# Experts ranked by token count: five passes of 96 slots and three of 64, written in line, rows returned once per round

## The chip, the cores and the metric

The kernel runs on one core of a Trainium2 chip. The metric is the device time of one execution in microseconds, median of several. The engines are TensorE (PE; its weight loads stand apart as PEld), VectorE (DVE), ScalarE (ACT), GpSimd (POOL) and SyncE (SP, which only issues DMAs). Each runs its own instruction stream, and they meet in semaphores.

## The reference

A trunk of two layers for 256 tokens of width 1024, all in float32. Layer 0 is windowed attention and a dense SwiGLU. Layer 1 is a Mamba-2 mixer and a mixture of experts, followed by a last norm. The change touches the mixture of experts alone:

```python
D_FF = 3584
N_EXPERTS = 8
TOP_K = 2
...
def moe_swiglu(h, w_router, w_gu, w_down):
    logits = (h @ w_router).astype(jnp.float32)
    top_v, top_i = lax.top_k(logits, TOP_K)
    gates = jax.nn.softmax(top_v, axis=-1)
    combine = jnp.sum(jax.nn.one_hot(top_i, N_EXPERTS, dtype=jnp.float32) * gates[..., None], axis=-2)
    ...
    for e in range(N_EXPERTS):
        out = out + combine[..., e:e + 1] * swiglu(h, w_gu[e], w_down[e])
    return out
```

The 512 choices (256 tokens, two each) are spread over eight experts. One expert's weights are 1024 x 7168 and 3584 x 1024 floats, 44 MB, and 352 MB for all eight.

## The kernel before

Up to about 562 us it runs layer 0 and the mixer of layer 1, with weights through a ring of six slots. Early in the dense SwiGLU, POOL clears two arrays in DRAM: `xg_rows`, the rows sent to the experts (L406), and `y_rows`, the rows that come back (L411). DVE waits for the clearing in front of L1731. Then comes the expert stage.

**The router** (DVE, L1817 to L1868) ranks the logits of each token and takes two. PE counts the tokens of each expert (L1233 to L1237). Each expert has 96 slots (`CAP`) in a round. Where one has more tokens, a second or third round of all eight experts follows; `last_i` says how many passes there are, less one. Every engine reads it into a register (L1249 on PE) and loops over the passes. The rows of expert 0 are picked by a matmul with a selection matrix (L1244), since nothing may wait for DRAM there; the others are scattered by POOL (L426) into `xg_rows`, and ACT loads those of the next expert in each pass (L741).

**A pass** (`expert`) handles one expert's 96 rows. The weights come as 48 chunks through `e_ring`, which has twelve slots of 128 x 2048 floats: 16 gate and up chunks of 1024 KB (set 0: 4 blocks of 512 columns), 16 of 768 KB (set 1: 4 blocks of 384), 12 down chunks of 1024 KB and 4 of 512 KB. SP issues the load of a chunk (L337) as soon as PE has used the one twelve before it (`chunk_used`). PE waits for a chunk on `e_loaded` (`have_e`).

The 96 rows are three groups of 32 (`QUAD`), and each matmul has 32 rows as its stationary side, at one of four positions of the array, so that four matmuls run beside one another. A gate or up chunk takes 12 matmuls (3 row groups x 4 blocks of columns), spread over three PSUM banks (L1283). A down k-tile takes 12 as well (L1301). The trace records each float32 matmul twice, so a pass has 768 records of L1283 and 672 of L1301. Between them PE transposes the hidden rows (L1274) and the next expert's rows (L1259); ACT does the Silu and moves the transposes, DVE multiplies gate by up (L1916), and both copy the down results to `yg`, which ACT stores to `y_rows` (L770).

**The loop.** All passes but the last are one loop body per engine (`Fori`; on PE L1341), and the last is written behind it. In the last pass POOL gathers the returned rows (L432 on) and DVE adds them with their gates (`rows_added`); the last expert's own rows stay in SBUF and come back by a matmul with `sel_last_T` (L1350). Then DVE adds that (L1947), ACT squares (L780), and the last norm follows. The vector of its gains, `gain_row`, is loaded in front of the last pass (L775).

Of the kernel before, what the change touches and what calls it, by code (L numbers as in the profile page):

```python
# [34 lines left out]
P = 128  # L35
T = 256
# [26 lines left out]
SLOT = 2048  # L63
CAP = 96
ROUNDS = -(-T // CAP)
QUAD = 32
# [4 lines left out]
CLEARED = ROUNDS * E * CAP // P + (ROUNDS - 1) * E + 1  # L71


def build(nc, x, positions, ln_mix, ln_ffn, ln_final, swa_w_qkv, swa_b_qkv, swa_sinks, swa_w_o,
# [11 lines left out]
    with ctx:  # L86
# [70 lines left out]
        first_slot = sb("first_slot", [P, TT, E])  # L157
# [26 lines left out]
        last_i = sb("last_i", [P, 1], I32)  # L184
        xg_rows = nc.dram_tensor("xg_rows", (ROUNDS * E, CAP, D), F32).ap()
        y_rows = nc.dram_tensor("y_rows", (ROUNDS * E, CAP, D), F32).ap()

# [47 lines left out]
        sel_last = cmp8[:].rearrange("p a t j -> p (a t j)").rearrange("p (t s) -> p t s", t=TT)[:, :, 0:CAP]  # L235
        sel_last_T = zeros[0:CAP, 0:T].rearrange("p (t s) -> p t s", t=TT)
# [10 lines left out]
        def at_quad(i):  # L247

            return slice(i % 4 * QUAD, (i % 4 + 1) * QUAD), i // 4, i // 3, slice(i % 3 * QUAD, (i % 3 + 1) * QUAD)
# [9 lines left out]
        def place_of(head):  # L259
# [31 lines left out]
        r_logit, r_max, r_exp, r_sel, r_cnt, r_passes, r_slots = map(  # L291
            sem, ("r_logit", "r_max", "r_exp", "r_sel", "r_cnt", "r_passes", "r_slots"))
# [9 lines left out]
        y_free, zeros_ready, rows_cleared = map(sem, ("y_free", "zeros_ready", "rows_cleared"))  # L302
# [9 lines left out]
        def _(sp):  # L312
# [53 lines left out]
        def _(pool_e):  # L366
# [11 lines left out]
            for i in range(NF):  # L378
                pool_e.memset(invf[:, i:i + 1], float(np.float32(THETA ** (-2.0 * i / ROT))))
            pool_e.iota(first_slot[:], [[0, TT], [CAP, E]], base=0, channel_multiplier=0,  # L380
                        allow_small_or_imprecise_dtypes=True)
# [18 lines left out]
            pool_e.wait_ge(f_gate, 1)  # L400
            pool_e.iota(column, [[1, P]], base=-int(FAR), channel_multiplier=0,
# [11 lines left out]
            pool_e.wait_ge(rows_cleared, 2 * CLEARED * 16)  # L413
# [15 lines left out]
            pool_e.wait_ge(r_passes, 1)  # L429
            last = pool_e.value_load(last_i[0:1, 0:1], min_val=E - 1, max_val=ROUNDS * E - 1)  # L430
            pool_e.sem_inc(y_free, 1)
            with pool_e.Fori(0, last) as it:  # L432
                pool_e.wait_ge(y_stored, it * 16 + 16)
                pool_e.sem_inc(y_free, 1)

            for i in range(2):
                if i == 1:
                    pool_e.wait_ge(y_added, TT)
                for t in range(TT):
                    pool_e.indirect_dma_start(xs[:, t], None, y_rows.rearrange("i p d -> (i p) d"),  # L440
                                              bass.IndirectOffsetOnAxis(slots_i[:, i, t:t + 1], 0)
                                              ).then_inc(y_got_in, 16)
# [3 lines left out]
        def _(act):  # L446
# [268 lines left out]
            act.wait_ge(r_passes, 1)  # L715
            last = act.value_load(last_i[0:1, 0:1], min_val=E - 1, max_val=ROUNDS * E - 1)
            act.sem_inc(y_act, 6)
            act.activation(root_table[:, 6:7], ones[:, 6:7], ACT.Silu)

            def expert(it, is_last):  # L720

                def gate(s, w):
                    act.wait_ge(chunk_used, it * LAYER_CHUNKS + (MOE0 + 16 * s + 8))
                    if s == 1:
                        act.wait_ge(m_h, 2 * it + 1)
                    for b in range(3):
                        ins = act.activation(m_sg[:, b, 0:w], bank[GATE[b]][:, 0:w], ACT.Silu)  # L727
                    ins.then_inc(m_silu, 1)

                def hidden_T(s, banks):  # L730
                    act.wait_ge(m_T, 2 * it + s + 1)
                    n = SETS[s][1] // P
                    for b in range(3):
                        ins = act.activation(m_hTs[s][:, :, b], bank[banks[b]][:, 0:n * P].rearrange("p (a n) -> p a n", a=n),  # L734
                                             ACT.Copy)
                    ins.then_inc(m_Tsb, 1)

                gate(0, 512)
                if not is_last:
                    act.wait_ge(rows_sent, 16 * 2 * TT)  # L740
                    act.dma_start(xg[0:CAP], xg_rows[it + 1]).then_inc(xg_loaded, 16)  # L741
# [3 lines left out]
                if is_last:  # L745
                    act.wait_ge(last_T, 1)
                    act.activation(sel_last_T, bank[UP[0]][0:CAP, 0:T].rearrange("p (t s) -> p t s", t=TT), ACT.Copy
                                   ).then_inc(last_sb, 1)
                    load_roots(4)
                else:  # L750
                    for i in range(2):
                        act.wait_ge(xg_T, it * 2 + (i + 1))
                        act.activation(xgT[:, 4 * i:4 * i + 4],
                                       bank[UP[i]][:].rearrange("p (a n) -> p a n", a=4)[:, :, 0:CAP],
                                       ACT.Copy).then_inc(xg_sb, 1)
                for b in range(3):
                    if b < 2:
                        act.wait_ge(m_y, it * 2 + (b + 1))
                    else:
                        act.wait_ge(chunk_used, it * LAYER_CHUNKS + (MOE0 + LAYER_CHUNKS))  # L760
                    if b == 0:
                        act.wait_ge(y_free, it + 1)
                    for q in (2, 3):
                        quad, _, d, rows = at_quad(4 * b + q)
                        act.activation(yg[rows, d * 256:(d + 1) * 256], bank[DOWN[b]][quad, 0:256], ACT.Copy  # L765
                                       ).then_inc(y_act, 1)
                if not is_last:
                    act.wait_ge(y_act, it * 6 + 12)
                    act.wait_ge(y_dve, it * 6 + 12)
                    act.dma_start(y_rows[it], yg[0:CAP]).then_inc(y_stored, 16)  # L770

            with act.Fori(0, last) as it:
                expert(it, False)
            act.wait_ge(rows_ready, TT)
            act.dma_start(gain_row, ln_final.partition_broadcast(P)).then_inc(gain_loaded, 16)  # L775
            expert(last, True)
            for n in range(2):
                for t in range(TT):
                    act.wait_ge(h_final, 2 * n + t + 1)
# [7 lines left out]
        def _(pe):  # L787
# [460 lines left out]
            pe.wait_ge(r_passes, 1)  # L1248
            last = pe.value_load(last_i[0:1, 0:1], min_val=E - 1, max_val=ROUNDS * E - 1)  # L1249

            def expert(it, is_last):
# [725 lines left out]
```

## Time and profile before

| | us |
|---|---|
| median of 3 runs | 1504.18 |
| lowest, highest | 1499.16, 1506.42 |
| the profiled execution | 1505.61 |
| its span, first to last instruction | 1503.8 |
| first matmul of an expert pass | 562.43 |
| first of the last products (L1350) | 1491.22 |

The profile is of one execution. Busy shares are of the span. "Issue" in the chain is time in which the engine waited for nothing that the profile shows. The granted clock is TensorE's, as a share of 2.4 GHz; the DMA share is the mean busy share of 16 DMA engines. The last column of a stretch is GB/s.

### The profile page before, as it was taken

Reading aid. Unit: us, or ns where it says so; the run is one execution under the profiler, and the core shown is the slowest. Engines: PE = TensorE matmul, PEld = TensorE weight load, DVE = VectorE, ACT = ScalarE, POOL = GpSimd, SP = SyncE. Lnnn points to the kernel's source line nnn. Section 1 sums busy time; section 2 is a strip of 40 time slices with the busy share of each in tenths; the row PEclk is TensorE's granted clock in tenths of the full one; section 3 lists DMA queues with packets and bytes.
Section 4 is the critical chain, followed back from the end, with each engine's and each line's share of the span. In section 5 each row is a group of like instructions: output and inputs, shape, how many; then the busy total and the mean of one; then the engine's idle time right before and its main releaser. Section 6 shows DMA issues by size and latency. Waiting matters only on the chain.

```text
span 1503.8 us, 33750 instructions
## 1 busy us (share of the span) xinstructions
PE 1461.4 (97%) x14996; PEld 863.8 (57%) x14996; DVE 427.8 (28%) x635; ACT 389.5 (26%) x590; POOL 81.8 (5%) x131
## 2 busy tenths in 40 slices
PE   8999999999999999999998999998999999999997
PEld 7688888888999873453462353353354344345344
DVE  6675554466899740000000000000000000001112
ACT  5654444346788530010000001000000000001011
POOL 2053000000012200000000000000000000000000
PEclk9999999999999999999999999999999999999999
DMA  9379855545544479999999999999999999999992
GB/s 336 120 271 409 314 182 185 190 157 169 160 121 141 141 266 378 371 397 397 359 405 375 345 414 399 343 410 383 337 405 396 362 407 391 371 400 387 423 419 109
DMA packets 132974, 471.55 MB, mean 314 GB/s; under 512 B 10080, under 2 KB 35952, under 8 KB 116448
## 3 DMA queue, kind: packets, MB, share of 16 engines
q1 hardware_dynamic: 123808, 440.44, 77.9%
q0 software_dynamic: 6624, 21.20, 3.6%
q10 hardware_dynamic: 2400, 7.70, 1.4%
q8 instruction: 127, 2.08, 0.5%
q14 instruction: 15, 0.12, 0.0%
HBM read 447.28 MB, written 22.02 MB: 312 GB/s over the span
## 4 chain that ended last, share of the span: by engine, by line
PE 82%; issue 12%; DVE 2%; POOLq 1%; DMA 1%; ACT 1%; DVEq 1%; SPq 0%; POOL 0%; ACTq 0%
PE bank L1283 39%; PE bank L1301 19%; PE bank L790 6%; PE bank L792 6%; PE bank L791 6%; PE bank L1274 1%; POOLq L421 1%; DMA ring<-swa_w_qkv_in 1%; DVE w_lo L1412 1%; POOLq L419 0%; PE bank L1012 0%; ACT w_hi L478 0%; PE bank L1259 0%; PE bank L815 0%; PE bank L1350 0%
## 5 line engine op out<-in xcount | busy, mean ns | idle before, releaser
L1283 PE MATMUL bank<-e_ring,xgT 128*32 128x512 f32 (+1 forms) x6144 | 591.9, 547 | 20.8 <-issue 20.8
L1283 PEld LDWEIGHTS bank<-e_ring,xgT 128*32 128x32 f32 x6144 | 198.4, 111 | 407.9 <-issue 407.6
L1412 DVE TENSOR_TENSOR w_lo<-ring,w_hi 128x2048 fp32r<-128x2048 f32 (+1 forms) x84 | 191.9, 2288 | 110.1 <-ACT w_hi L478 109.8
L478 ACT ACTIVATE w_hi<-ring 128x2048 fp32r<-128x2048 f32 (+1 forms) x84 | 158.8, 1895 | 127.4 <-PE bank L792 118.7
L1916 DVE TENSOR_TENSOR m_hh<-m_sg,bank 128x512 f32<-128x512 f32 (+1 forms) x48 | 26.9, 616 | 577.5 <-PE bank L1283 577.5
L1301 PE MATMUL bank<-e_ring,m_hT_a 128*32 128x256 f32 x3072 | 168.9, 379 | 0.0
L1301 PEld LDWEIGHTS bank<-e_ring,m_hT_a 128*32 128x32 f32 x3072 | 99.0, 110 | 67.2 <-issue 3.3
L790 PE MATMUL bank<-w_hi,hT_hi 128*128 128x512 f32 (+1 forms) x336 | 131.1, 390 | 2.1 <-DVE w_lo L1412 1.7
L792 PE MATMUL bank<-w_hi,hT_lo 128*128 128x512 f32 (+1 forms) x336 | 129.2, 384 | 0.0
L791 PE MATMUL bank<-w_lo,hT_hi 128*128 128x512 f32 (+1 forms) x336 | 129.1, 384 | 0.0
L1301 PE MATMUL bank<-e_ring,m_hT_b 128*32 128x256 f32 x2304 | 125.8, 379 | 0.0
L1301 PEld LDWEIGHTS bank<-e_ring,m_hT_b 128*32 128x32 f32 x2304 | 74.9, 110 | 49.4
L1938 DVE COPY yg<-bank 32x256 f32<-32x256 f32 x48 | 19.9, 415 | 276.5 <-PE bank L1301 275.8
L727 ACT ACTIVATE m_sg<-bank 128x512 f32<-128x512 f32 (+1 forms) x48 | 22.7, 545 | 241.3 <-PE bank L1283 241.3
L790 PE MATMUL bank<-hT_hi,w_hi 128*128 128x256 f32 x256 | 73.1, 286 | 0.9 <-DVE w_lo L1412 0.9
L790 PEld LDWEIGHTS bank<-w_hi,hT_hi 128*128 128x128 f32 x336 | 63.1, 188 | 16.2 <-DVE w_lo L1412 2.4
L792 PE MATMUL bank<-hT_hi,w_lo 128*128 128x256 f32 x256 | 72.4, 283 | 0.0
L791 PE MATMUL bank<-hT_lo,w_hi 128*128 128x256 f32 x256 | 72.4, 283 | 0.0
L734 ACT ACTIVATE m_hT_a<-bank 128x512 f32<-128x512 f32 x24 | 12.6, 599 | 225.5 <-PE bank L1274 225.5
L792 PEld LDWEIGHTS bank<-w_hi,hT_lo 128*128 128x128 f32 x336 | 63.1, 188 | 12.8
L791 PEld LDWEIGHTS bank<-w_lo,hT_hi 128*128 128x128 f32 x336 | 63.2, 188 | 11.9
L765 ACT ACTIVATE yg<-bank 32x256 f32<-32x256 f32 x48 | 18.1, 376 | 184.3 <-PE bank L1301 183.8
(330 smaller groups left out, 1232.8 us busy)
## 6 DMA issues: line engine op xcount, KB each, us to landing
e_ring<-moe_w_gu_in SPq DMA_DIRECT2D x128, 1024.0 KB, 7.4
e_ring<-moe_w_gu_in SPq DMA_DIRECT2D x128, 768.0 KB, 6.5
e_ring<-moe_w_down_in SPq DMA_DIRECT2D x96, 1024.0 KB, 10.8
ring<-ffn_w_gu_in SPq DMA_DIRECT2D x28, 1024.0 KB, 8.9
e_ring<-moe_w_down_in SPq DMA_DIRECT2D x32, 512.0 KB, 10.1
ring<-ffn_w_down_in SPq DMA_DIRECT2D x14, 1024.0 KB, 4.9
xg_rows<-zeros POOLq DMA_DIRECT2D x36, 256.0 KB, 12.3
ring<-ssm_w_in_in SPq DMA_DIRECT2D x8, 1024.0 KB, 5.0
```

The costliest lines, as they stand in the source:

```text
L421: pool_e.drain()
L478: act.activation(w_hi[:, m % SPLIT, 0:w], ring[:, m % RING, 0:w], ACT.Copy).then_inc(hi_ready, 1)
L727: ins = act.activation(m_sg[:, b, 0:w], bank[GATE[b]][:, 0:w], ACT.Silu)
L765: act.activation(yg[rows, d * 256:(d + 1) * 256], bank[DOWN[b]][quad, 0:256], ACT.Copy).then_inc(y_act, 1)
L790: pe.matmul(o, stat[0], mov[0], start=start, stop=False)
L791: pe.matmul(o, stat[0], mov[1], start=False, stop=False)
L792: return pe.matmul(o, stat[1], mov[0], start=False, stop=stop)
L1283: ins = pe.matmul(bank[banks[b]][quad, 0:w], xgT[:, k, rows], e_ring[:, c % ERING, block_n * w:(block_n + 1) * w], start=(k == 0), stop=(k ...
L1301: ins = pe.matmul(bank[DOWN[b]][quad, 0:256], hT_at[:, a, i // P, i % P:i % P + QUAD], e_ring[:, (32 + c) % ERING, (k - k0) * D + d * 256: ...
L1412: dve.tensor_tensor(w_lo[:, m % SPLIT, 0:w], ring[:, m % RING, 0:w], w_hi[:, m % SPLIT, 0:w].bitcast(F32), ALU.subtract).then_inc(lo_ready, 1)
L1916: ins = dve.tensor_tensor(m_hh[:, b, 0:w], m_sg[:, b, 0:w], bank[UP[b]][:, 0:w], ALU.mult)
L1938: dve.tensor_copy(yg[rows, d * 256:(d + 1) * 256], bank[DOWN[b]][quad, 0:256]).then_inc(y_dve, 1)
```

## The change

Experts are ranked on the chip by their token counts. Expert 0 always ranks first (its first chunks are loaded before the counts are known). The five that rank highest take passes of 96 slots, the other three passes of 64, which have two row groups in place of three. The passes stand in the set order of ranks 0, 5, 1, 2, 6, 3, 4, 7, so sizes are 96, 64, 96, 96, 64, 96, 96, 64. `order_i` tells SP which expert's weights each pass needs, `rounds_i` tells all engines how many rounds there are. The loop goes over rounds, and its body holds the eight passes in line. The returned rows are gathered and added once per round, in its last pass, so `y_rows` needs room for one round and less of it is cleared. `gain_row` is loaded before the loop. The last product sits in the loop, and ACT waits for all of `back_mm` before it leaves.

```diff
+SMALL = 64
+RANK_AT = (0, 5, 1, 2, 6, 3, 4, 7)
+LARGE = 5
+GROUPS = tuple(CAP // QUAD if r < LARGE else SMALL // QUAD for r in RANK_AT)
...
         @block.sync
...
-            sp.wait_ge(r_passes, 1)
-            last = sp.value_load(last_i[0:1, 0:1], min_val=E - 1, max_val=ROUNDS * E - 1)
+            sp.wait_ge(r_order, 1)
+            rounds = sp.value_load(rounds_i[0:1, 0:1], min_val=1, max_val=ROUNDS)
+            last = sp.snap(rounds * E - 1, min_val=E - 1, max_val=ROUNDS * E - 1)
             with sp.Fori(0, last) as it:
-                expert_loads(it, it % E, ERING, LAYER_CHUNKS)
-                expert_loads(it + 1, (it + 1) % E, 0, ERING)
-            expert_loads(last, E - 1, ERING, LAYER_CHUNKS)
+                here = sp.value_load(order_i[0:1, bass.ds(it % E, 1)], min_val=0, max_val=E - 1)
+                expert_loads(it, here, ERING, LAYER_CHUNKS)
+                following = sp.value_load(order_i[0:1, bass.ds(it % E + 1, 1)], min_val=0, max_val=E - 1)
+                expert_loads(it + 1, following, 0, ERING)
...
         @block.gpsimd
...
-            for i in range(E - 1, ROUNDS * E):
-                for a in range(2):
-                    pool_e.dma_start(y_rows[i][:, 512 * a:512 * (a + 1)], zeros[0:CAP, :]
-                                     ).then_inc(rows_cleared, 16)
...
+            for p in range(E):
+                filled = rows_of(p) if p < E - 1 else 0
+                if filled < CAP:
...
+            with pool_e.Fori(0, rounds) as it:
+                pool_e.wait_ge(r_back, it + 1)
+                pool_e.wait_ge(y_stored, it * (16 * (E - 1)) + 16 * (E - 1))
...
         @block.scalar
...
+            act.wait_ge(rows_ready, TT)
+            act.dma_start(gain_row, ln_final.partition_broadcast(P)).then_inc(gain_loaded, 16)
+            act.wait_ge(r_rounds, 1)
...
+            with act.Fori(0, rounds) as it:
+                for p in range(E):
+                    expert(it, p)
+                act.wait_ge(back_mm, it * (2 * TT) + 2 * TT)
...
         @block.tensor
...
                 def up_or_gate(c, s, banks):
                     w, k = SETS[s][1], c % 8
                     have_e(c)
-                    for b in range(3):
+                    for b in range(groups):
                         for q in range(4):
...
+                pe.wait_ge(xg_loaded, it * (16 * E) + 16 * (p + 1))
+                if p == E - 1:
+                    pe.wait_ge(last_ready, it + 1)
                 hidden_T(1, GATE)
-                if is_last:
+                if p == E - 1:
                     shares_T()
-                else:
-                    rows_T()
+                rows_T()
...
-            with pe.Fori(0, last) as it:
-                expert(it, False)
-            expert(last, True)
...
+            with pe.Fori(0, rounds) as it:
+                for p in range(E):
+                    expert(it, p)
+                pe.wait_ge(last_sb, it + 1)
+                pe.wait_ge(xg_sb, it * (2 * E) + (2 * E + 2))
...
+                pe.wait_ge(h_final, it * (2 * TT) + 4 * TT)
...
         @block.vector
...
+            dve.scalar_tensor_tensor(key, counts, float(E), key_bias[:], ALU.mult, ALU.add)
...
+            dve.tensor_reduce(rank, rank_is, AXX, ALU.add)
...
+            dve.tensor_scalar(small, rank, LARGE - 0.5, float(CAP - SMALL), ALU.is_gt, ALU.mult)
...
+            dve.tensor_scalar(rounds_i[:], rk[:, 8, 0:1], 1.0, None, ALU.add).then_inc(r_rounds, 1)
```

On PE, at the end of the first pass. Before, where L1301 are the last down matmuls and L1283 the next pass's first gate matmuls:

```order
L1301 MATMUL bank7<-e_ring,m_hT_b 32x256 x16
L1301 MATMUL bank5<-e_ring,m_hT_b 32x256 x16
L1341 REGISTER_ALU
L1341 COMPARE_AND_BRANCH
L1312 ISA
L1254 ISA
L1283 MATMUL bank0<-e_ring,xgT 32x512 x4
L1283 MATMUL bank1<-e_ring,xgT 32x512 x4
L1283 MATMUL bank2<-e_ring,xgT 32x512 x4
```

And now, with a pass of two row groups behind it:

```order
L1351 MATMUL bank7<-e_ring,m_hT_b 32x256 x16
L1351 MATMUL bank5<-e_ring,m_hT_b 32x256 x16
L1362 REGISTER_ALU
L1305 REGISTER_ALU
L1333 MATMUL bank0<-e_ring,xgT 32x512 x4
L1333 MATMUL bank1<-e_ring,xgT 32x512 x4
```

The branch is gone from between the passes, and a chunk has eight matmuls in two banks in place of twelve in three.

On DVE, between the selection of the first rows and the number that the loops wait for. Before:

```order
L1848 TENSOR_TENSOR rt<-rt 128x16
L1850 TENSOR_REDUCE rt<-bank0 128x1
L1852 TENSOR_SCALAR rt<-bank7 128x16 x2
L1854 TENSOR_TENSOR rt<-rt,st 128x16
L1856 TENSOR_SCALAR rt<-rt 128x1 x2
L1857 TENSOR_TENSOR rt<-rt,first_slot 128x16
L1858 TENSOR_TENSOR rt<-rt,bank7 128x16
L1860 TENSOR_TENSOR rt<-rt 128x1
L1861 TENSOR_TENSOR rt<-rt 128x16
L1863 TENSOR_SCALAR last_i<-rt 128x1
```

Now, from the ranks on (`rk` holds ranks, sizes and reaches):

```order
L1908 TENSOR_REDUCE rk<-cmp8 128x8
L1909 TENSOR_TENSOR rt<-rt,st 128x16
L1911 TENSOR_SCALAR rk<-rk 128x8
L1913 TENSOR_SCALAR choice<-rt 128x16 x2
L1915 TENSOR_TENSOR rk<-bank0,rk 128x8
L1916 TENSOR_TENSOR rt<-bank7,rk 128x16
L1918 TENSOR_TENSOR rk<-rk 128x8
L1919 TENSOR_SCALAR rk<-rk 128x8
L1921 SCALAR_TENSOR_TENSOR rk<-rk 128x8
L1923 TENSOR_REDUCE rk<-rk 128x1
L1925 TENSOR_SCALAR rounds_i<-rk 128x1
```

The ranking stands ahead of the number of rounds, and the order of the experts and the slots follow behind it.

On ACT, at the end of the program. Before, the squares stand right behind the last copies to `yg`:

```order
L765 ACTIVATE yg<-bank5 32x256 x2
L780 ACTIVATE xs,rt<-h 128x512 x4
```

Now the wait for the last products and the loop's branch stand between:

```order
L814 ACTIVATE yg<-bank7 32x256 x2
L824 ISA
L821 REGISTER_ALU
L821 COMPARE_AND_BRANCH
L827 ISA
L828 ACTIVATE xs,rt<-h 128x512
```

## Rows read from the trace of the kernel before

**Rows 1.** The page: busy shares; moved bytes in 40 equal slices

```profile
PE 1461.4 (97%) x14996; PEld 863.8 (57%) x14996; DVE 427.8 (28%) x635; ACT 389.5 (26%) x590; POOL 81.8 (5%) x131
...
GB/s 336 120 271 409 314 182 185 190 157 169 160 121 141 141 266 378 371 397 397 359 405 375 345 414 399 343 410 383 337 405 396 362 407 391 371 400 387 423 419 109
```

**Rows 2.** Busy time by stretch: passes 1, 2, 3, 8; passes 2 to 8

```profile
core 0: us, PE busy (x) PEld busy (x) DVE busy (x) ACT busy (x) POOL busy (x), PEclk, DMA share, GB/s
562.50:674.60 112.10, 112.09 (x1469) 49.39 (x1469) 5.48 (x11) 10.00 (x22) 3.97 (x4) 1.00 0.98 379
674.60:791.15 116.55, 113.85 (x1469) 50.42 (x1469) 5.86 (x12) 8.70 (x20) 0.00 (x0) 0.99 0.99 385
791.15:910.88 119.73, 114.80 (x1470) 49.09 (x1469) 5.86 (x12) 8.69 (x20) 0.00 (x0) 0.97 0.99 378
...
1379.71:1491.22 111.51, 111.51 (x1465) 48.87 (x1456) 12.43 (x27) 9.67 (x21) 3.83 (x4) 1.00 0.85 349
...
674.60:1491.22 816.62, 795.81 (x10278) 346.14 (x10278) 47.58 (x99) 61.81 (x141) 3.83 (x4) 0.98 0.98 379
```

**Rows 3.** Chain that ended last: start us, length us, what

```profile
674.59 2.71 issue
677.30 50.84 PE bank L1283 x480
729.60 23.36 PE bank L1283 x288
752.96 10.36 PE bank L1301 x192
765.12 26.04 PE bank L1301 x480
...
1379.71 48.94 PE bank L1283 x480
```

**Rows 4.** PE loop's branch by line; stretch behind the first jump back

```profile
L1341 PEldq COMPARE_BRANCH  x7: 83/3802/5972, 673.2 to 1378.4; - x7
...
678.60:682.00 3.40, 3.40 (x20) 0.90 (x16) 0.00 (x0) 0.00 (x0) 0.00 (x0) 0.50 0.96 360
```

**Rows 5.** Waits of SP in the expert stage: us in total, times, longest

```profile
SPq L337 <- PE bank L1283: 465.0, 256, 8.7
```

**Rows 6.** DMA from 1390 to 1470 us: 40 slices, packets, one group of issues

```profile
GB/s 436 414 434 418 422 422 434 412 429 425 421 423 421 421 433 421 424 429 415 417 422 421 426 417 418 419 422 422 416 410 426 422 420 420 412 418 422 414 420 422
DMA packets 7164, 33.71 MB, mean 421 GB/s; under 512 B 637, under 2 KB 637, under 8 KB 6499
...
e_ring<-moe_w_down_in SPq DMA_DIRECT2D x12, 1024.0 KB, 14.1
```

**Rows 7.** Busy time by stretch: two stretches of lower rate

```profile
674.60:690.00 15.40, 12.70 (x104) 3.90 (x108) 0.83 (x2) 0.75 (x2) 0.00 (x0) 0.89 0.98 386
...
1050.00:1100.00 50.00, 50.00 (x536) 17.54 (x532) 1.88 (x3) 4.41 (x9) 0.00 (x0) 1.00 0.97 347
```

**Rows 8.** DVE and PE by time at the router; PE's register load by line

```profile
558.07 0.16 DVE L1844 TENSOR_REDUCE rt<-rt 128x2 f32<-128x16 f32 x1
...
559.81 0.15 DVE L1863 TENSOR_SCALAR last_i<-rt 128x1 int32<-128x1 f32 x1
...
L1249 PEldq TENSOR_LOAD <-last_i x1: 485/485/485, 560.3 to 560.3; - x1
...
562.43 1.07 PE L1283 MATMUL bank<-e_ring,xgT 128*32 128x512 f32 x8
```

**Rows 9.** ACT's last squares by line: min/median/max ns, first and last start

```profile
L780 ACT ACTIVATE xs<-h x4: 629/630/630, 1493.0 to 1495.6; 128x512 f32<-128x512 f32 x4
```

**Rows 10.** Clearing of y_rows, and VectorE behind its wait, by line

```profile
L411 POOL DMA_DIRECT2D y_rows<-zeros x34: 512/512/555, 110.6 to 127.3; - x34
...
L1731 DVE TENSOR_SCALAR zeros<-arg,sm x1: 474/474/474, 383.8 to 383.8; 128x384 f32<-128x384 f32 x1
```

More of the change, by code:

```diff
@@ L763, in expert @@
+                for b in range(GROUPS[p]):
+                    if b < GROUPS[p] - 1:
+                        act.wait_ge(m_y, it * m_y_before(E) + (m_y_before(p) + b + 1))
+                    else:
+                        act.wait_ge(chunk_used, it * (E * LAYER_CHUNKS) + (MOE0 + (p + 1) * LAYER_CHUNKS))
+                    if b == 0 and p > 0:
+                        act.wait_ge(y_stored, it * (16 * (E - 1)) + 16 * p)
                     for q in (2, 3):
-                        quad, _, d, rows = at_quad(4 * b + q)
@@ L1279, in up_or_gate @@
                     have_e(c)
-                    for b in range(3):
+                    for b in range(groups):
                         for q in range(4):
-                            quad, _, block_n, rows = at_quad(4 * b + q)
+                            quad, _, block_n, rows = at_quad(p, 4 * b + q)
                             ins = pe.matmul(bank[banks[b]][quad, 0:w], xgT[:, k, rows],
@@ L1290, in down @@
                         have_e(32 + c)
[L1291 removed]
+                    for b in range(groups):
                         if chunks[0] == 0 and b == 2:
[L1293 removed]
+                            pe.wait_ge(m_h, it * (2 * E) + (2 * p + 2))
                         for c in chunks:
@@ new lines, in _ @@
+            dve.tensor_tensor(based, rank_is, base_at[:].unsqueeze(1).to_broadcast([P, E, E]), ALU.mult)
+            dve.drain()
+            dve.tensor_reduce(rk[:, 9], taken, AXX, ALU.add)
+            dve.tensor_reduce(base, based, AXX, ALU.add)
+            dve.tensor_scalar(r2[6], r2[6], CAP - 0.5, None, ALU.is_gt)
+            dve.tensor_scalar(step, small, float(ROUND_ROWS - CAP), None, ALU.add)
+            dve.drain()
+            dve.tensor_copy(order_i[:, 0:E], rk[:, 9])
+            dve.tensor_copy(order_i[:, E:E + 1], rk[:, 9, 0:1]).then_inc(r_order, 1)
@@ L1938, in expert @@
                         dve.tensor_copy(yg[rows, d * 256:(d + 1) * 256], bank[DOWN[b]][quad, 0:256]).then_inc(y_dve, 1)
-            with dve.Fori(0, last) as it:
-                expert(it, False)
-            expert(last, True)
-            for n in range(2):
-                for t in range(TT):
-                    dve.wait_ge(back_mm, 2 * n + t + 1)
-                    hh = h[:, t, 512 * n:512 * (n + 1)]
-                    dve.tensor_tensor(hh, hh, bank[2 * n + t][:], ALU.add).then_inc(h_final, 1)
+            with dve.Fori(0, rounds) as it:
+                for p in range(E):
+                    expert(it, p)
+                for n in range(2):
+                    for t in range(TT):
+                        dve.wait_ge(back_mm, it * (2 * TT) + (2 * n + t + 1))
+                        hh = h[:, t, 512 * n:512 * (n + 1)]
+                        dve.tensor_tensor(hh, hh, bank[2 * n + t][:], ALU.add).then_inc(h_final, 1)
```

359 lines of the change are left out of this document (208 added, 151 removed).

## The prediction

> **What bounds the kernel now.** I read the shares first. TensorE (PE) is busy for 97% of the span, and the moved bytes rise to a plateau near 400 GB/s in the last two thirds, where the experts run [rows 1]. The reader is to see two limits close together, so the next question is how each behaves pass by pass. The table of passes [rows 2] shows eight passes from 562.50 to 1491.22 us (928.7 us): the first takes 112.1, the six after it 116.3 to 119.7 (three of them are shown), the last 111.5, at 379 GB/s over the last seven.
>
> The chain of pieces says what a pass is made of [rows 3]. The matmuls of the last pass begin with 48.94 us; in the second the same 480 take 50.84, after 2.71 us of "issue". The rest (23.36 + 10.36 + 26.04) repeats exactly in every pass. So the passes of the loop lose 5 to 8 us each at their start. The loop's own branch tells why [rows 4]: seven executions, one of 83 ns (the exit) and a median of 3.8 us, up to 6.0, when it goes back. Behind it the granted clock is 0.50 (1.2 instead of 2.4 GHz) for 3.4 us. Over the stage 928.7 - 8 x 111.5 = 36.7 us are lost, nearly all behind the six jumps back.
>
> PE never waits for weights in this stage, since SyncE (SP) waits for PE: 465 us in 256 waits on the gate and up matmuls alone [rows 5]. Yet DMA is not far off. In the last pass transfers queue up (12 down transfers take a median of 14.1 us to land) and the 16 engines move 421 GB/s for 80 us, gathers included [rows 6]. A pass holds 44 MB of weights (per pass 16 transfers of 1024 KB and 16 of 768 KB, 12 of 1024 KB and 4 of 512 KB), so at 421 it needs 104.6 us: only 7 us under PE's 111.5.
>
> **The change, part by part.**
>
> Passes in line. Six jumps back go; between passes two register operations stand where the branch stood. The exit without a jump cost no idle time (the last pass starts at 1379.71, right behind the one before) [rows 3]. For PE alone that is -36.7 us.
>
> Three passes of 64 rows. PE issues 8 instead of 12 matmuls per chunk or k-tile. The matmul pieces of a clean pass are 48.94 + 23.36 + 10.36 + 26.04 = 108.7 us [rows 3]; two thirds are 72.5, and with the 2.8 us of transposes left in 111.5 a small pass is 75.3 us of PE. PE alone would need 5 x 111.5 + 3 x 75.3 = 783.4 us, 145.3 less than now.
>
> Weights. They don't shrink: every pass still loads all 44 MB. A small pass uses them at 44 / 75.3 = 585 GB/s, which no stretch shows. So the end is now set by the stream. The first pass is large, has its twelve chunks in the ring, and stays PE's: it ends near 674.6 us. From there to the end the kernel before moved 0.379 x 816.6 = 309.2 MB [rows 2]. The changed one moves 0.5 MB less for gain_row (loaded in the first pass now), 0.3 MB less of stored rows (two stores of 64 instead of 96), and 0.1 MB more of loaded rows (seven loads, 608 rows, instead of six, 576): 308.5 MB. At 421 GB/s these are 732.8 us. Does the stream ever stop for want of a slot? The first small pass is next; it empties the lead (in the first pass PE is some 7 chunks behind the landings, about 18 us, against 104.6 - 75.3 = 29 us that it overtakes). Each large pass wins back 7 us, two in a row 14, and the ring holds twelve chunks (29 us). So it never fills again, and the last pass is a small one, which ends with the stream. Loads end at 675.0 + 732.8 = 1407.8; behind the last landing PE has two half chunks in two groups, 8/12 of 2 x 1.3 us = 1.7: 1409.5, against 1491.2. **-81.7 us.** The 145 us of PE's saving are thus worth 82, and the loop's 37 are inside them: of these two edits either would be hidden partly by the other's limit.
>
> The rate's bounds: 436 GB/s (the best slice of the 80 us) gives 707.6 us, 25 less; 386 GB/s, the first 15.4 us after the first pass [rows 7], where few transfers are in flight, gives 799.2, 66 more. I take 421, since twelve slots freed at once are most like the queued last pass.
>
> On the page a rule speaks against this. The Trainium skill, DMA: Bandwidth & Descriptors, section Where 436 GB/s comes from, says that for HBM to SBUF the memory side binds at about 358 GB/s per core. The trace disagrees on this core alone: 421 for 80 us. By the page's figure the 308.5 MB would take 862 us, and the kernel would end near 1554 us, slower than before.
>
> Router on VectorE. After the selection of the first rows the kernel before needs four dependent steps from 558.07 to 559.81 us for last_i [rows 8], 0.37 to 0.5 us each. Now there are nine groups up to rounds_i, so about 561.2. PE read it into a register at 560.3 (485 ns) and had about 1 us in hand before its first expert matmul at 562.43, which stood behind the first rows' matmuls anyway. rounds_i is 1.4 us later, so that matmul comes some 0.4 us late (0 to 2). **+0.4** (in the 675.0 above). order_i follows 1.5 us later, near 562.9, and SP first needs it for the thirteenth chunk, whose slot is free at 565.2. Slots come about 3 us later, hence the scatter too; the load of the second expert's rows is issued behind the first Silu at 583.5 and used after 640: hidden. The gates move ahead of the loop, to where VectorE idles until 603: nothing. If the scatter came over 15 us late it would hold ScalarE.
>
> SP now reads one register per half pass (PE's such read took 485 ns). With up to twelve transfers queued this is covered; it would cost if the queue were empty.
>
> Tail. The four squares on ScalarE ran in step with VectorE's additions, the last one from 1495.6 [rows 9]. Now ScalarE waits for all four back products first, then leaves the loop: the squares (0.86 us apart) start near 1495.2 instead of 1493.0. **+2.0 us** (1 to 3). PE's added wait for h_final has nothing behind it. The added transposes of the next round's rows stand in the last pass, under the stream.
>
> Clearing. 70 DMAs of zeros become 44. They were issued by 127 us and are first awaited before 383.8 us [rows 10]: nothing either way. New iota and memset instructions on GpSimd stand ahead of them, equally covered.
>
> Sum: -81.7 + 2.0 = **-79.7 us**. The profiled execution took 1505.6 (span 1503.8 and 1.8 around it), which gives 1425.9; against the median of 1504.2, 1424.5. I say 1425.
>
> **The rivals.**
>
> A slower stream. Twelve transfers in flight, a hungry PE, stores, gathers and code on the same engines: if it runs at 390 to 403 GB/s, the loads take 765 to 791 us and the time is 1457 to 1483. For it: the 386 and the 347 of one 50 us stretch [rows 7]; against it: those are stretches with few transfers in flight.
>
> Slower than before, by the stream. Break-even is at 308.5 / 812.5 us = 380 GB/s. At 354 GB/s, between the slow stretches (347 and 357) [rows 7], the loads take 871 us: 1563. The Trainium skill's page named above (DMA: Bandwidth & Descriptors) stands beside this case with its 358. Against it: the whole loop ran at 379 while SP was held back by PE.
>
> Slower than before, by the clock. In a starved small pass PE works 1.7 us of every 2.5. If the clock then stayed at 1.2 GHz, a small pass would take 150.6 us and the stage 111.9 + 4 x 111.5 + 3 x 150.6 = 1009.7: +81 and +2.0, 1587. It decides where a small pass is over 122 us. Against it: at half the clock a chunk takes 3.4 us, more than the stream's 2.5, so PE would be busy without a gap, and such stretches ended after 3.4 us [rows 4]. Shorter cold stretches cost nothing, since they lie inside the wait.
>
> PE remains the bound. This needs 308.5 MB in 672 us, 459 GB/s; it would give 1504.2 - 145.3 + 2.4 = 1361.
>
> The change doesn't do what it says. More than one round is run if an expert has more tokens than its slots. From the reference's inputs I work out 56, 50, 82, 56, 57, 84, 62, 65 for experts 0 to 7. Expert 0 is always first; 84, 82, 65 and 62 take the other large passes, 57, 56 and 50 the small ones: one round. A second would add eight passes of 104.6, about 2260 us in all.
>
> **How the numbers follow.** Forecast 0.77; slower stream 0.13; PE the bound 0.03; no change, a stream at just about 380, 0.03; the two slower cases 0.02 and 0.01, a second round 0.01. The range runs from 1403 (nearly the 436 bound) to 1462 (a rate of 401), which leaves out the far half of the slower stream and the rest. Faster 0.93, within 0.5% 0.03, slower 0.04; 0.5% is about what a measurement of this kernel can tell.
>
> **What would show it.** Right: the first pass about 112 us; small passes of 85 to 105 us, the last the longest; no pass starting behind an idle time of 2.7 us without a landing at its end; waits of PE for e_ring in the small passes; 415 to 425 GB/s from 675 us on; SP waiting far less; squares that start only behind the last back product. Wrong: a rate under 400 with eight or more chunks in flight, a granted clock near 0.5 through a small pass with PE fully busy, or a gap at passes' starts while chunks lie ready.

## The result, and the profile after

The changed kernel takes 1440.43 us (median of 4 runs, 1437.92 to 1446.04) against 1505.30 for the kernel before on the same chips: ratio 0.9573, 95% interval 0.952 to 0.9626. It is 64.9 us faster. 1425 was forecast, inside a range of 1403 to 1462. The profiled execution is the fastest of the four: 1437.92 us, its span 1436.2.

The page of the changed kernel, with the lines that answer to [rows 1]: busy shares, and in 40 equal slices the granted clock (in tenths), DMA's busy share and the moved bytes.

```profile
span 1436.2 us, 30954 instructions
...
PE 1360.0 (95%) x13543; PEld 812.3 (57%) x13543; DVE 425.9 (30%) x646; ACT 383.5 (27%) x575; POOL 69.4 (5%) x116
...
PEclk9999999999999999999999999999999999999998
DMA  9369655556543446999999999999999999999994
GB/s 349 119 231 407 212 182 187 188 174 183 156 131 123 172 170 259 407 401 380 414 420 425 413 420 424 414 420 421 416 420 425 414 419 424 414 412 393 412 420 193
```

PE has lost 101 us of work and the kernel 65. From the second pass on most slices of moved bytes now stand between 412 and 425 GB/s, with one at 393, where [rows 1] goes up and down between 337 and 423.

The busy time by stretch, one stretch for each of the eight passes and then passes 2 to 8 together up to the last landing; it answers to [rows 2] and has its columns.

```profile
560.98:673.05 112.07, 112.07 (x1473) 49.52 (x1477) 10.29 (x30) 11.07 (x23) 3.97 (x4) 1.00 0.97 382
673.05:766.94 93.89, 81.44 (x983) 32.69 (x974) 3.81 (x8) 6.14 (x14) 0.00 (x0) 0.98 1.01 410
766.94:881.23 114.29, 112.64 (x1473) 50.62 (x1477) 6.00 (x13) 8.75 (x21) 0.00 (x0) 1.00 1.02 419
881.23:993.16 111.93, 111.93 (x1474) 49.42 (x1469) 5.86 (x12) 8.48 (x20) 0.00 (x0) 1.00 1.02 419
993.16:1091.37 98.21, 80.64 (x982) 31.44 (x974) 3.82 (x8) 6.15 (x14) 0.00 (x0) 1.00 1.02 419
1091.37:1205.15 113.78, 112.58 (x1473) 49.43 (x1477) 6.00 (x13) 8.75 (x21) 0.00 (x0) 1.00 1.02 420
1205.15:1317.07 111.92, 111.92 (x1473) 49.42 (x1469) 5.86 (x12) 8.48 (x20) 0.00 (x0) 1.00 1.01 412
1317.07:1421.92 104.85, 83.68 (x985) 31.71 (x976) 10.04 (x19) 7.88 (x17) 3.84 (x4) 0.97 0.94 382
673.05:1419.85 746.80, 692.90 (x8793) 293.60 (x8784) 40.70 (x81) 53.93 (x123) 3.84 (x4) 0.99 1.01 413
```

The five large passes take 111.9 to 114.3 us, where those of the loop took 116.3 to 119.7 [rows 2]. The three small ones take 93.9, 98.2 and 104.9 and not the 75 that PE works in them.

The branch of the PE loop by its line (count, ns min/median/max, first and last start):

```profile
L1392 PEldq COMPARE_BRANCH  x1: 97/97/97, 1426.7 to 1426.7; - x1
```

And the longest waits of PE in the whole program (us in total, times, longest):

```profile
PE bank L1333 <- DMA e_ring<-moe_w_gu_in: 29.4, 56, 2.2
PE bank L1351 <- DMA e_ring<-moe_w_down_in: 24.5, 21, 3.6
PE bank L838 <- DVE w_lo L1464: 3.2, 4, 0.9
```

Against [rows 4] the branch is there once, as an exit. Instead of the idle "issue" of [rows 3] PE now waits 53.9 us for weights. The timeline of PE in the first small pass shows how: 16 records of a chunk take 1.5 us, then PE waits some 0.33 us for the next landing (in brackets: the idle time before the row and what ended it).

```profile
712.93 1.50 PE L1333 MATMUL bank<-e_ring,xgT 128*32 128x384 f32 x16 [0.31 <-DMA e_ring<-moe_w_gu_in]
714.77 1.50 PE L1333 MATMUL bank<-e_ring,xgT 128*32 128x384 f32 x16 [0.34 <-DMA e_ring<-moe_w_gu_in]
716.58 1.50 PE L1333 MATMUL bank<-e_ring,xgT 128*32 128x384 f32 x16 [0.31 <-DMA e_ring<-moe_w_gu_in]
```

SP's waits for PE in passes 2 to 8 are also shorter. On the gate and up matmuls they are less than half of the 408.1 us that the same passes had before (the 465.0 of [rows 5] has the first pass in it):

```profile
SPq L368 <- PE bank L1333: 172.3, 129, 3.0
SPq L368 <- PE bank L1351: 81.2, 46, 3.3
```

So the place of the bound moved as the prediction said, from PE and its loop to the weights' stream, and the small passes wait for it. What remained to test: that the jumps really cost what I put on them, that the stream and nothing else holds the small passes, and why it ran at 413 and not 421 GB/s.

### The profile page after: what moved, and what is told of

It reads as the page before. It is cut to its first block, busy times and chain, and to the rows that moved or that the text cites. A ratio compares the mean times of both kernels' runs of the same rounds, so it can differ in the third digit from the quotient of the medians.

```text
span 1436.2 us, 30954 instructions
## 1 busy us (share of the span) xinstructions
PE 1360.0 (95%) x13543; PEld 812.3 (57%) x13543; DVE 425.9 (30%) x646; ACT 383.5 (27%) x575; POOL 69.4 (5%) x116
## 4 chain that ended last, share of the span: by engine, by line
PE 62%; DMA 15%; issue 11%; SPq 6%; DVE 2%; POOLq 2%; ACT 1%; DVEq 1%; POOL 0%; ACTq 0%
PE bank L1333 25%; PE bank L1351 13%; DMA e_ring<-moe_w_gu_in 9%; PE bank L838 7%; PE bank L840 7%; PE bank L839 7%; SPq L368 5%; DMA e_ring<-moe_w_down_in 5%; POOLq L467 1%; PE bank L1324 1%; DMA ring<-swa_w_qkv_in 1%; DVE w_lo L1464 1%; POOLq L465 0%; PE bank L1060 0%; ACT w_hi L525 0%
## 5 line engine op out<-in xcount | busy, mean ns | idle before, releaser
L1333 PE MATMUL bank<-e_ring,xgT 128*32 128x384 f32 (+1 forms) x5376 | 522.2, 542 | 29.5 <-DMA e_ring<-moe_w_gu_in 29.4
L1333 PEld LDWEIGHTS bank<-e_ring,xgT 128*32 128x32 f32 x5376 | 167.6, 110 | 377.0 <-issue 290.1
L2020 DVE TENSOR_TENSOR m_hh<-m_sg,bank 128x512 f32<-128x512 f32 (+1 forms) x42 | 23.7, 616 | 530.9 <-PE bank L1333 530.9
L1351 PE MATMUL bank<-e_ring,m_hT_a 128*32 128x256 f32 x2688 | 151.6, 385 | 12.8 <-DMA e_ring<-moe_w_down_in 12.8
L1351 PEld LDWEIGHTS bank<-e_ring,m_hT_a 128*32 128x32 f32 x2688 | 90.5, 111 | 71.7 <-issue 17.2
L1351 PE MATMUL bank<-e_ring,m_hT_b 128*32 128x256 f32 x2016 | 113.0, 380 | 11.7 <-DMA e_ring<-moe_w_down_in 11.7
L1351 PEld LDWEIGHTS bank<-e_ring,m_hT_b 128*32 128x32 f32 x2016 | 65.0, 110 | 58.8 <-DMA e_ring<-moe_w_down_in 11.1
L783 ACT ACTIVATE m_hT_b<-bank 128x384 f32<-128x384 f32 x21 | 8.9, 491 | 207.6 <-PE bank L1324 207.6
## 6 DMA issues: line engine op xcount, KB each, us to landing
e_ring<-moe_w_down_in SPq DMA_DIRECT2D x32, 512.0 KB, 15.4
```

The lines of the kernel that those rows point to most:

```text
L1333: ins = pe.matmul(bank[banks[b]][quad, 0:w], xgT[:, k, rows], e_ring[:, c % ERING, block_n * w:(block_n + 1) * w], start=(k == 0), stop=(k ...
L1351: ins = pe.matmul(bank[DOWN[b]][quad, 0:256], hT_at[:, a, i // P, i % P:i % P + QUAD], e_ring[:, (32 + c) % ERING, (k - k0) * D + d * 256: ...
L2020: ins = dve.tensor_tensor(m_hh[:, b, 0:w], m_sg[:, b, 0:w], bank[UP[b]][:, 0:w], ALU.mult)
```

## Experiments

Theory A is that of the prediction: a pass costs PE 111.5 or 75.3 us, a jump back costs 3 to 5 us of idle time and a cold clock, and from the first small pass on the stream sets the end. The rivals are named in each expectation.

**The changed kernel again**, on the same chip as the next two and as the kernel whose first pass is small.

> The changed kernel itself, beside the three others of this call. Both theories expect what was measured: 1440 us (1436 to 1446).

Measured: 1438.34 us (1437.07 to 1442.51, 4 runs); ratio to before 0.957 (0.9532 to 0.9607).

**Seven large passes, one small.** The passes in line, with hardly any work taken away.

```diff
-LARGE = 5
+LARGE = 7
```

> The changed kernel with seven passes of 96 slots and one of 64, the last: the passes in line nearly alone. Theory A (the loop's jumps cost the 36.7 us, and a large pass in line is PE's own 111.5 us, with the stream just behind it): the first seven passes end at 561.0 + 112.1 + 6 x 111.7 = 1343 us, the last takes 97 (the stream), and the time is 1343 + 97 + 2 + 16 = 1458 us. Rival B (large passes are held by the weights, the jump only hid that): the passes stay at the 116.6 us of before, and the time is 1488 us or more. Under B no large pass is near 112.

Measured: 1460.54 us (1458.13 to 1464.65), ratio 0.972 (0.9681 to 0.9759). Passes 2 to 7 together, and the second pass alone:

```profile
672.92:1344.59 671.67, 671.67 (x8818) 298.20 (x8814) 35.15 (x72) 51.91 (x120) 0.00 (x0) 1.00 1.01 402
672.92:784.87 111.95, 111.95 (x1473) 49.72 (x1469) 5.86 (x12) 8.69 (x20) 0.00 (x0) 1.00 1.01 405
```

Six large passes in line take 671.67 us, 111.9 each, with PE busy all the time at full clock. The six of the loop took 116.3 to 119.7, 705.1 together (674.60 to 1379.71). So the jumps were worth 33.4 us, and rival B falls. The last, small pass took 98 us. By the medians passes in line and one small pass are worth 43 us together, and the other two small passes 22 more. The 402 GB/s here is no limit of the stream: it is what PE takes when it never waits.

**Padding.** Idle work on PE at each pass's end, about as long as a jump's gap.

```diff
+PAD = 32
...
                 for chunks in down_groups(p):
                     down(chunks)
+                for _ in range(PAD):
+                    pe.transpose(bank[GATE[0]][:, 0:P], m_hh[:, 0, 0:P], ident[:])
```

> The changed kernel with 32 idle transposes of 128x128 on PE at the end of every pass, about 4.1 us each time by the 0.128 us of the twelve at L1274, about as much as a jump back cost. Theory A (from the first small pass on the weights' stream sets the end): only the first pass's and the last pass's padding can reach the end, +4 to +8 us, 1444 to 1448 us. Rival B (PE's work still adds up): 8 x 4.1 = +33 us, 1473 us.

Measured: 1443.43 us (1442.41 to 1451.38), 5.1 over the changed kernel beside it. A stretch of 116 us that begins 2 us before the padding in front of the fourth pass (a large one) and ends before the next padding, and all after the first pass:

```profile
881.00:997.00 116.00, 116.00 (x1513) 52.98 (x1509) 5.86 (x12) 8.47 (x20) 0.00 (x0) 1.00 1.01 410
...
673.00:1421.00 748.00, 711.68 (x9016) 317.88 (x9015) 40.68 (x81) 53.88 (x123) 3.84 (x4) 1.00 1.01 412
```

The padding took 3.7 us each time and not the 4.1 expected, 30 us in all. With it the fourth pass took 115.7 us (its first matmul at 886.62, the next pass's at 1002.33). By the medians 5 us reached the end, close to one padding behind the last pass. So where three passes are small, PE time of the size of the jumps costs next to nothing; the jumps were worth their full price only in the kernel before. This adds work, not jumps; small passes in a loop of their own were not tried.

**Half the weights' bytes.** From the thirteenth chunk on, in the changed kernel and in the one before:

```diff
+                if short:
+                    half = dst.shape[2] // 2
+                    dst, src = dst[:, :, 0:half], src[:, :, 0:half]
                 sp.dma_start(dst, src).then_inc(e_loaded[c % ERING], 16)
```

> The changed kernel, but from the thirteenth chunk on each weight transfer brings only the first half of every row of its chunk (PE multiplies what the slot held before in the other half, so the result is not the reference's). Theory A (PE's own work is 111.5 us for a large and 75.3 for a small pass, and only the stream holds it): 561.0 + 112.1 + 4 x 111.5 + 3 x 75.3 = 1345 us at the end of the passes, 1361 us in all, small passes of 75 to 76 us, no wait for e_ring. Rival B (small passes are held by something else too, by the copies of ACT and DVE or by a low clock after gaps): small passes of 85 us or more, 1390 us or more.

Measured: 1363.8 us (2 runs). The first small pass, the second, and the large pass before the latter:

```profile
674.90:749.94 75.04, 75.04 (x986) 33.22 (x982) 3.80 (x8) 6.12 (x14) 0.00 (x0) 1.00 0.89 304
...
861.89:973.82 111.93, 111.93 (x1474) 49.45 (x1469) 5.86 (x12) 8.47 (x20) 0.00 (x0) 1.00 0.66 204
...
973.82:1048.86 75.04, 75.04 (x986) 33.22 (x982) 3.81 (x8) 6.13 (x14) 0.00 (x0) 1.00 0.88 302
```

The prediction had 75.3 and 111.5 us. With fewer bytes and nothing else changed the small passes fall to PE's own time at full clock, so the bytes held them, and ACT and DVE did not. The stream costs the changed kernel about 1440 - 1364 = 76 us (medians from different chips).

> The kernel before with the same halved transfers (its result is not the reference's either). Theory A (the gap at a pass's start is the jump back and its fetch of code, which the weights' traffic only lengthens): six gaps of 2 to 3 us remain, with the cold clock behind them, the passes take 114 to 116.5 us and the time is 1485 to 1503 us. Rival B (the gaps are transfers that come late): no gap, 111.5 us each, 1468 us.

Measured: 1495.64 us (1494.30 to 1500.14, 8 runs), ratio 0.9967 (0.9939 to 0.9995). The loop's branch by its line:

```profile
L1344 PEldq COMPARE_BRANCH  x7: 83/3404/3744, 671.4 to 1367.1; - x7
```

PE's idle time behind it, from the list of waits:

```profile
PE bank L1286 <- issue: 14.5, 6, 2.6
```

And its second pass by the busy time of a stretch:

```profile
672.75:787.16 114.41, 112.16 (x1469) 50.06 (x1469) 5.86 (x12) 8.69 (x20) 0.00 (x0) 1.00 0.66 201
```

With half the bytes all six gaps remain, 2.4 us each and not 3.5, and the longest branch takes 3.7 and not 6.0 us [rows 4]. So the gap belongs to the jump, and the weights' traffic lengthens it, by 6 us over six jumps. The cold clock doesn't always follow: the second pass here ran at full clock behind a gap of 2.3 us, the other five gaps were followed by 3.4 us at 1.2 GHz each. Why the jump costs that much isn't shown. It isn't the price of any loop: in the kernel before SP's own loop (L355) jumps back in 45 ns.

**All passes small.**

```diff
-LARGE = 5
+LARGE = 0
...
-            dve.tensor_scalar(rounds_i[:], rk[:, 8, 0:1], 1.0, None, ALU.add).then_inc(r_rounds, 1)
+            dve.tensor_scalar(rounds_i[:], rk[:, 8, 0:1], 0.0, 1.0, ALU.mult, ALU.add).then_inc(r_rounds, 1)
```

> The changed kernel with all eight passes of 64 slots and the number of rounds set to one (tokens past an expert's 64th are left out, so the result is not the reference's). Theory A (the stream alone sets the end when the first pass is small too): PE's work falls by another 5 x 36 = 180 us and the time stays within 5 us of the kernel whose first pass is small (1432): 1427 to 1434 us, eight passes of which those after the first take 104 to 107 us. Rival B (PE's work still counts in large passes, which win the stream's lead): 1400 us or less.

Measured: 1426.39 us (1423.88 and 1428.91). Its second pass, and all from there to 1400 us:

```profile
652.67:759.66 106.99, 84.42 (x983) 30.70 (x982) 3.86 (x9) 5.92 (x14) 0.00 (x0) 0.98 1.02 419
...
652.67:1400.00 747.33, 586.31 (x6781) 215.52 (x6780) 33.25 (x66) 42.82 (x99) 3.85 (x4) 0.98 1.01 418
```

Some 180 us of PE work less gives 12 to 14 us (1426.4 against 1438.3 and 1440.4, medians from different chips), and half of that comes with a small first pass alone, as the next run shows. It is just under the 1427 to 1434 expected. So as long as all eight experts are loaded in this way, another division of the rows among passes of 96 and 64 has little left to win.

**First pass small.** The first pass is PE's in the changed kernel, and the stream runs at 382 GB/s during it.

```diff
-RANK_AT = (0, 5, 1, 2, 6, 3, 4, 7)
+RANK_AT = (7, 0, 1, 5, 2, 3, 4, 6)
...
-            pool_e.memset(key_bias[:, 0:1], FAR)
+            pool_e.memset(key_bias[:, 0:1], -FAR)
```

> Expert 0 always ranks last in place of first and takes a pass of 64; sizes 64, 96, 96, 64, 96, 96, 96, 64, still five and three. Theory A (the stream sets the end wherever PE is ahead of it; the first pass, PE's, let it run at 382 instead of 418 GB/s): the stream is at full rate some 112 us longer, which is worth (418 - 382) / 418 x 112 = 10 us, and 2 for the slow start of the second pass: 1428 us. Rival B (PE's sum sets the end): the same five large and three small passes, the same 1440 us. Rival C (the order of sizes matters only by the lead that is left over at the end): the last pass is small as before, no change either.

Measured: 1432.49 us (1432.15 to 1440.45), ratio 0.9543 (0.95 to 0.9586), 5.9 us under the changed kernel on the same chip. The intervals of the two ratios overlap, so the gain isn't secured. The profile shows its cause: the first pass's last chunk is used at 652.99 us and the last pass ends at 1415.99, where the changed kernel has 673.05 and 1421.92. Of the 20 us that the first pass gives, 6 are left at the end. I had put 12 on it.

**A ring of eight chunks.**

```diff
-ERING = 12
+ERING = 8
```

> The changed kernel with a ring of eight chunks for the experts' weights instead of twelve. Theory A (the rate of the stream follows from how many transfers are in flight): in large passes two or three are in flight and not five, these run at 380 GB/s or less, and the first small pass starts with four chunks less landed: +10 us for that lead and up to +25 for the rate, 1455 to 1475 us. Rival B (the rate doesn't depend on the depth once PE takes chunks as they come): +10 us alone, 1450 us, and the stretches behind the first small pass stay at 418 GB/s.

Measured: 1456.64 us (1454.79 and 1458.49). Passes 3, 4, 5 and 7, and all after the first pass:

```profile
774.94:892.12 117.18, 113.52 (x1473) 50.15 (x1477) 6.00 (x13) 8.74 (x21) 0.00 (x0) 1.00 1.01 403
892.12:1004.05 111.93, 111.93 (x1474) 49.43 (x1469) 5.86 (x12) 8.48 (x20) 0.00 (x0) 1.00 1.01 405
1004.05:1106.93 102.88, 81.80 (x983) 30.57 (x974) 3.82 (x8) 6.14 (x14) 0.00 (x0) 1.00 1.01 412
...
1222.18:1334.12 111.94, 111.94 (x1473) 49.43 (x1469) 5.86 (x12) 8.48 (x20) 0.00 (x0) 1.00 1.00 402
...
673.40:1440.20 766.80, 698.87 (x8792) 291.44 (x8784) 40.69 (x81) 53.89 (x123) 3.85 (x4) 0.99 1.01 407
```

20 us more from the start of the second pass to the last landing. About half is the smaller lead: 312.3 MB still had to come, against 308.3. The other half is the rate, 407 against 413 GB/s. It shows in passes 3 and 5, where PE waits for weights: 403 and 412, against 419 in both with twelve slots. Passes 4 and 7 take PE's own 111.9 us, so their 405 and 402 are PE's pace and no limit of the stream. So the depth does tell on the rate, in theory A's direction; but my 380 was too low by more than 20. DMA's busy share is 1.00 to 1.02 in both kernels, so that share doesn't tell.

**Squares in the loop.** The edit is made on top of the small first pass, and the kernel with that first pass alone was measured once more beside it. The edit of the first pass stands above and is left out here.

```diff
-                act.wait_ge(back_mm, it * (2 * TT) + 2 * TT)
-            for n in range(2):
-                for t in range(TT):
-                    act.wait_ge(h_final, rounds * (2 * TT) + (2 * n + t + 1))
+                for n in range(2):
+                    for t in range(TT):
+                        act.wait_ge(h_final, it * (2 * TT) + (2 * TT + 2 * n + t + 1))
...
+                pool_e.wait_ge(sq_final, it * 4)
...
-            dve.wait_ge(sq_final, 4)
+            dve.wait_ge(sq_final, rounds * 4)
```

> The kernel whose first pass is small, and with the four squares of the last norm inside the loop, each behind its own addition as before the change, in place of behind the wait for all four last products. Theory A (that wait costs what the tail grew by: from the first last product to the last square 5.8 us against 4.4 before the change): -1.4 us against the kernel whose first pass is small, 1431 us. Rival B (the loop's exit on ScalarE, now behind the squares, costs as much): the same time. In the profile the first square starts about 1.9 us behind the first last product instead of 4.0.

> The kernel whose first pass is small, once more, beside the one with early squares: 1432 us.

Measured: 1432.54 us (1430.55 to 1435.99, 6 runs), ratio 0.9546 (0.952 to 0.9573), and 1434.05 us (1431.91 to 1440.88), ratio 0.9557 (0.9529 to 0.9585), for the one without. The difference has the expected size and is inside the noise. In the traces the squares are seen. Without the edit, in the timeline of ACT of the kernel whose first pass is small, the idle time before the first of them is ended by the last product, L1401, whose first began at 1416.18:

```profile
1420.15 0.63 ACT L828 ACTIVATE xs<-h 128x512 f32<-128x512 f32 x1 [3.32 <-PE bank L1401]
...
1422.01 0.61 ACT L828 ACTIVATE xs<-h 128x512 f32<-128x512 f32 x1
```

With it, in the same view, by DVE's addition, where the first product began at 1417.31:

```profile
1419.19 0.63 ACT L828 ACTIVATE xs<-h 128x512 f32<-128x512 f32 x1 [1.23 <-DVE h L2053]
```

From the first product to the last square it is 5.8 us without and 4.5 with the edit (the last square there starts at 1421.77). The kernels with a small first pass, with this edit (1432.5) and without (1432.5 and 1434.1), are the fastest of those that compute all: 4 to 6 us under the 1438.3 of the changed one.

## Why the prediction came out as it did

**What bounds the kernel: right.** Two limits close together, and the loop's jumps on top. The seven large passes in line show PE's 111.9 without a gap and put 33.4 us on the jumps, where 36.7 was forecast; the halved transfers show that the gaps are the jumps'.

**PE's own time: right.** 75.3 forecast, 75.04 measured with the stream out of the way; 111.5 against 111.9.

**The stream sets the end from the first small pass on: right.** Small passes of 85 to 105 us were forecast, the last the longest; they took 93.9, 98.2 and 104.9. The padding and the eight small passes leave no more than a few us to PE's work: one padding of eight, and 6 us for the 145 us by which all small passes and a small first pass differ.

**The sum: 12 us short of the profile.** -79.7 us was forecast against the profiled execution's 1505.6; it was 1437.9 - 1505.6 = -67.7 (by the medians 64.9). The terms:

| | forecast | measured | difference |
|---|---|---|---|
| start of the second pass | 675.0 | 673.05 | -1.95 |
| from there to the last landing | 732.8 | 746.8 | +14.0 |
| last landing to the first last product | 1.7 | 2.3 | +0.6 |
| from there to the end of the span | 14.6 | 14.1 | -0.5 |

**The mis-sized term is the time of the stream.** The bytes were right (308.5 MB forecast; 308.3 MB up to the end of the last pass). The step that failed reads: "I take 421, since twelve slots freed at once are most like the queued last pass." One 80 us stretch, with the queue full, stood for 747 us. The stream after, cut in five (the fourth row comes before the third in time):

```profile
673.05:700.00 26.95, 26.11 (x241) 7.33 (x232) 0.83 (x2) 1.84 (x4) 0.00 (x0) 1.00 0.99 382
700.00:1300.00 600.00, 567.98 (x7288) 245.42 (x7292) 28.86 (x58) 43.40 (x100) 0.00 (x0) 1.00 1.02 418
1340.00:1410.00 70.00, 54.92 (x679) 22.24 (x680) 7.09 (x8) 5.33 (x11) 1.89 (x2) 0.98 1.02 421
1300.00:1340.00 40.00, 37.72 (x496) 15.80 (x484) 3.92 (x13) 3.35 (x8) 1.96 (x2) 0.96 1.00 391
1410.00:1420.00 10.00, 6.20 (x106) 2.86 (x100) 0.00 (x0) 0.00 (x0) 0.00 (x0) 1.00 0.45 181
```

Each stretch's loss against 421 is its length times the missing share: 27 x 39/421 = 2.5 us, 600 x 3/421 = 4.3, none, 40 x 30/421 = 2.9, and 10 x 240/421 = 5.7 us; 15.4 in all, for a difference of 14.0.

Shorter stretches say where the rate is lost:

```profile
673.05:679.00 5.95, 5.95 (x61) 1.81 (x56) 0.83 (x2) 0.75 (x2) 0.00 (x0) 1.00 0.93 302
679.00:691.00 12.00, 12.00 (x120) 3.62 (x114) 0.00 (x0) 1.09 (x2) 0.00 (x0) 1.00 1.01 421
691.00:695.00 4.00, 4.00 (x44) 1.07 (x36) 0.00 (x0) 0.00 (x0) 0.00 (x0) 1.00 1.03 337
793.00:797.00 4.00, 3.18 (x32) 0.78 (x24) 0.00 (x0) 0.00 (x0) 0.00 (x0) 1.00 1.01 330
797.00:850.00 53.00, 52.68 (x651) 22.68 (x655) 3.36 (x6) 2.83 (x6) 0.00 (x0) 1.00 1.02 422
```

The 421 itself was right: between the dips the stream runs at 421 to 423 GB/s for 50 to 110 us at a time up to 1230 us, and again from 1340 to 1410. Three things were priced at nothing:

- The loads of the next expert's rows (`xg`, 384 or 256 KB, issued by ACT at L791). Seven of them fall behind the first pass, and during the later part of each the total falls to 313 to 354 GB/s for 3 to 5 us, with 9 to 11 weight transfers in flight in six of the seven and 8 or 9 in the other. They cost 5.4 us together. The 80 us that gave the 421 have no such load. The changed kernel's other trace has the same seven dips. That they come from the row loads is read from their times and wasn't tested.
- The starts of the first and of the last small pass: 302 GB/s for 6 us here, 311 for 5 us from 1317; 3 us together. The rows of the large pass before are being stored then, and three to seven weight transfers are in flight at the first, six to eight at the last. The first 5 to 6 us of the other passes run at 406 to 422 in this trace, with such a store too, so neither the store nor the short queue alone explains it, and the cause stays open. The 386 of [rows 7], which I used as a bound only, is such a start. The late part of the second of two large passes is slow as well: 391 for 15 us from 1294.
- The drain. From 1410 us on the rate falls, and the last four small transfers still land one after the other until 1419.85. I had counted the stream at full rate to the last byte.

"Wrong: a rate under 400 with eight or more chunks in flight" was one of my signs. It came true for some 27 us in all, in the row loads, and not for the stream as a whole.

**Router, SP's reads, clearing: right in effect.** PE went from the first rows' last matmul to its first expert matmul without a gap, where +0.4 us was forecast (0 to 2). The stage began 1.5 us earlier than in the profile before; the experiments' traces scatter as much, and the kernel before with halved transfers began as early, so I don't count it for the change. So 1.5 of the 2 us by which the second pass began early are luck.

**Tail: right in kind.** +2.0 us forecast, 1.5 measured (14.1 against 12.6). The squares in the loop show that the wait for all products is its cause.

**Rivals.** "A slower stream" began at 403 GB/s; the 413 measured lies about half way to it from 421. The stream kept 418 GB/s for 600 us and 413 over 747 us. The Trainium skill's 358 (DMA: Bandwidth & Descriptors, Where 436 GB/s comes from), which that section gets by halving the memory's rate between two cores, did not hold for this core running alone. At the first down chunks of each small pass PE stood idle for 3.5 us (it waits for two transfers at once there). With that the granted clock fell to 1.2 GHz for 3.4 us in two of the three passes, from 735.9 us (1.3 us after PE went on) and from 1387.8 (0.8 before it did), and not in the one at 1058; at 1336.6 us it fell behind 2.2 us of idle time. It cost nothing that reached the end, since PE waited for the next landing again behind each of them. PE as the bound and a second round did not occur.

**Two slips in the working**, without weight: 0.379 x 816.6 is 309.5, while the 309.2 MB that I went on with is the trace's own count; and the 357 GB/s set beside the 347 is not in [rows 7] but in 4 us of the last pass before (1382 to 1386).

## What to carry to other kernels

When two limits stand within a few per cent, price a saving on one by the other: here 145 us of PE's work and jumps were worth 65, and DMA's busy share of 98% before had not meant that DMA held the kernel. Work out the other resource's time for the bytes that remain, with its rate in each phase: at the start with few transfers in flight, in the middle with the other loads that run beside it, and in the drain. A rate taken from one quiet stretch is the best case. A jump back of PE's loop cost it 2.3 to 4.9 us of idle time (3.5 in the mean before, 2.4 with half the bytes), with 3.4 or 6.8 us of cold clock behind eleven of the twelve; the same passes in line ran without a gap.

## What the runs showed that I had not expected

- The busy share of DMA was 0.98 at 379 GB/s and 1.02 at 421, and 1.03 in the 4 us at 337. It is no measure of the rate. The depth of the queue tells something of it: 403 and 412 GB/s with a ring of eight in passes where PE waits, 419 in the same passes with twelve. But it isn't all: the dips at the row loads have 8 to 11 transfers in flight.
- The last 10 us of the stream ran at 181 GB/s in the profiled execution and at 186 in the kernel of eight small passes, but at 272 in the changed kernel's other trace and at 289 in the one whose first pass is small. So the drain costs 3 to 6 us in these four and varies between runs of one kernel; a second trace of the small first pass has 393. Why the last transfers land so late while DMA time is idle stays open: the profile doesn't tell the 16 engines apart, and a division of the last chunks into other sizes wasn't tried.
- SP's issue of a down chunk itself took 2.1 us in the median and up to 6.3, and 0.33 at best:

```profile
L368 SPq DMA_DIRECT2D e_ring<-moe_w_down_in x112: 333/2067/6298, 711.5 to 1403.0; - x112
```

Meanwhile slots stood free for up to 11 us, so I'd expect more slots to deepen the queue by less than their number; that wasn't tried. What makes an issue slow stays open: slow ones stood behind 7 transfers in flight as well as behind 11. SP's reads of `order_i` (0.27 us each) are hidden, since at least three transfers were in flight at every issue of passes 2 to 8.
